# RWKV scan: products over four tiles of the array, copies for additions, and a first product in two parts

## The chip, the core and the metric

One core of a Trainium2 chip runs the whole program. The time is that of the device in microseconds, the median of three runs. The profile is one further execution of the same kernel, with a time of its own.

## What is computed

Two transformer blocks over 256 latent and 256 context tokens at width 1024, in fp32. The change lies in the second block's RWKV mixer: 8 heads of 64 channels, two directions, 512 tokens. Its recurrence, over tokens:

```python
def wkv7_scan(state0, r, w, k, v, a_vec, b_vec, reverse):
    xs = tuple(t.transpose(1, 0, 2, 3) for t in (r, w, k, v, a_vec, b_vec))

    def step(S, inp):
        r_t, w_t, k_t, v_t, a_t, b_t = inp
        sa = jnp.einsum('bhij,bhj->bhi', S, a_t)
        S = (S * w_t[:, :, None, :] + sa[..., None] * b_t[:, :, None, :]
             + v_t[..., None] * k_t[:, :, None, :])
        return S, jnp.einsum('bhij,bhj->bhi', S, r_t)

    s_fin, ys = lax.scan(step, state0, xs, reverse=reverse)
    return s_fin, ys.transpose(1, 0, 2, 3)
```

The kernel doesn't step through tokens. It takes 128 tokens at once: the matrix M of a chunk (how token s acts on token t, strictly triangular) enters as the inverse of (1 - M), and this inverse is built by halves: for blocks of width 1, 2, 4, ..., 64, with X the inverse so far, X becomes X + X (M masked to this level) X. There are seven levels.

## The kernel before

`Rwkv` (from L2434) has 32 units of work: 4 chunks of 128 tokens, times 4 pairs of heads, times 2 directions (`todo`). `run` (L2674) is called once for each engine and writes out that engine's queue by hand: a loop over rounds, where every fifth round (`APART`) starts a unit, and each running unit, oldest first, issues one round's share of its work. Four units run at a time (`NS`), each with a set of buffers. A unit of phase p stands in its round p. So queues are strictly in the order round, then age of the unit, and a wait at the head of a queue holds the other three units' work too.

A unit's rounds: ScalarE forms the decays EB and EI (phase 1); VectorE forms RA and KB (2); TensorE forms four matrices, KB against RA, 64x128 tiles of 256 columns, and transposes KB (3); VectorE masks the products into MM (`copy_predicated`, L173), ScalarE takes the diagonal blocks out as MC (3). Then the levels, i = 0 to 6: in phase 4 + 2i TensorE forms T = ML^T X0 (ML is MC masked by GpSimd), ScalarE copies T to T1, and in phase 5 + 2i TensorE forms T1^T X1 and X1^T T1 (the group called xx), which VectorE adds to XX, the pair of the inverse X0 and its transpose X1. The last level joins the two 64-token halves (XF). Then wu0 (16), wu1 (18), the state's update st and the output y (19). VectorE scales the state by the chunk's decay and writes y.

Two heads lie in the two halves of the partitions. Every 64x64 product of a level reads one half and writes the same half, so the groups use two of the array's four 64x64 tiles. PSUM's eight banks are given in turn (`Banks.take`, L251), and `free` makes TensorE wait until the bank's former content was read. `close_*` (L2698) end the readout of a pair of heads from round 146 on (`CLOSE`).

The level's products before:

```python
for hh in range(2):
    for b in both:
        ins = e.matmul(ps[b, hh * 64:(hh + 1) * 64], ML[b, hh, :], XX[b, 0, hh, :] if i else self.IC[b, :], True, True)
```

Of the kernel before, what the change touches and what calls it, by code (L numbers as in the profile page):

```python
# [240 lines left out]
class Banks:  # L241


    def __init__(self, tiles):
        self.tiles, self.n, self.bank, self.before, self.emptied = tiles, 0, {}, {}, {}
        self.inside = [None] * len(tiles)

    def again(self):
        self.n, self.inside = 0, [None] * len(self.tiles)

    def take(self, key):  # L251
        assert not Flag.counting[0] or key not in self.bank, key
        b = self.n % len(self.tiles)
        self.n += 1
        self.bank[key], self.before[key] = b, self.inside[b]
        self.inside[b] = key
        return self.tiles[b]

    def free(self, key):
        k = self.before[key]  # L260
        if k is None or Flag.counting[0]:
            return []
        return self.emptied[k]

    def of(self, key):
        return self.tiles[self.bank[key]]

# [73 lines left out]
class Kit:  # L341


    def __init__(self, nc, dram, outer):
# [5 lines left out]
        self.banks = Banks([outer.enter_context(nc.psum_tensor(f"ps{i}", [P, 512], F32)) for i in range(8)])  # L350
# [2083 lines left out]
class Rwkv:  # L2434
# [18 lines left out]
    def late(self, st):  # L2453
# [15 lines left out]
        size = dict(EB=[P, 129], RA=[P, 256], KBt=[P, 2, P], MM=[P, 2, 512], WU=[P, 2, P], XF=[P, 2, P], XX=[P, 2, 2, 64],  # L2469
                    T1=[P, 2, 64], sm=[P, 3])  # L2470
        self.sets, at = [{}], 0
        for k, s in size.items():
            n = int(np.prod(s[1:]))
            view = self.A[:, at:at + n]
            self.sets[0][k] = view if len(s) == 2 else view.rearrange("p (a n) -> p a n", a=2) if len(s) == 3 else \
                view.rearrange("p (a b n) -> p a b n", a=2, b=2)
            at += n
# [3 lines left out]
        for B in self.sets:  # L2481
            B["MC"], B["ML"] = (B["WU"][:, q, :].rearrange("p (h n) -> p h n", h=2) for q in range(2))
            B["EI"] = B["T1"].rearrange("p a n -> p (a n)")
            B["KB"] = B["XX"].rearrange("p q h n -> p q (h n)")
# [62 lines left out]
    def pe(self, e, beside, amid):  # L2547
# [29 lines left out]
        S.meet(e, p, "prep")  # L2577
        self.run(e, self.unit_pe, self.close_pe, amid)
        S.meet(e, p)
# [78 lines left out]
    def pool(self, e):  # L2658
# [3 lines left out]
        for b in (slice(0, 64), slice(64, 128)):  # L2662
# [5 lines left out]
            e.wait_ge(*o.now())  # L2668
        for B in self.sets:
            e.memset(B["XF"][:, :, :], 0.0).then_inc(*o.up("compact"))  # L2670
        self.run(e, self.unit_pool)
        S.meet(e, S.pool)

    def run(self, e, unit, close=None, beside=None):  # L2674


        running, closing = [], []
        for r in range(self.CLOSE[-1] + 4):
# [3 lines left out]
            for u in list(running):  # L2682
                if next(u, "over") == "over":
                    running.remove(u)
            assert len(running) <= self.NS
# [5 lines left out]
            if beside is not None:  # L2691
                beside(e, r)

# [87 lines left out]
    def unit_pe(self, e, n, step, d, j, B):  # L2781
# [6 lines left out]
        yield  # L2788
        yield
        yield  # L2790
        got = []
        for hh in range(2):
            got.append(g.banks.take(("mm", n, hh)))
            for tok in g.banks.free(("mm", n, hh)):
                e.wait_ge(*tok)
        e.wait_ge(*S.dve.at(("kb", n)))
        for q in range(2):
            for hh, b in enumerate(both):
                ins = e.matmul(got[hh][:, q * 256:(q + 1) * 256], KB[b, q, :], RA[b, :], True, True)
                if q:  # L2800
                    ins.then_inc(*p.up(("mm", n, hh)))
# [6 lines left out]
        yield  # L2808
        for i, li in self.levels():
            yield  # L2810
            key = ("lev", n, i)
            ps = g.banks.take(key)
            for tok in g.banks.free(key):
                e.wait_ge(*tok)
            if i:
                e.wait_ge(*S.dve.at(("x", n, i - 1)))
            if li:
                e.wait_ge(*S.pool.at(("ml", n, i)))
                e.wait_ge(*S.pool.at("compact"))
                for hh in range(2):  # L2820
                    for b in both:
                        ins = e.matmul(ps[b, hh * 64:(hh + 1) * 64], ML[b, hh, :], XX[b, 0, hh, :] if i else self.IC[b, :], True, True)
            else:
                for hh in range(2):
                    ins = e.matmul(ps[dst, hh * 64:(hh + 1) * 64], MM[src, hh, dst], XX[src, 0, hh, :], True, True)
            ins.then_inc(*p.up(("t", n, i)))
            if li == 0:
                self.wu0_pe(e, n, RA, MM, state, v)
            if i:
                yield  # L2830
                key = ("xx", n, i)
                ps = g.banks.take(key)
                for tok in g.banks.free(key):
                    e.wait_ge(*tok)
                e.wait_ge(*S.act.at(("t", n, i)))
                if li:
                    for hh in range(2):
                        for b in both:
                            e.matmul(ps[b, 128 + hh * 64:192 + hh * 64], T1[b, hh, :], XX[b, 1, hh, :], True, True)
                    for hh in range(2):  # L2840
                        for b in both:
                            ins = e.matmul(ps[b, hh * 64:(hh + 1) * 64], XX[b, 1, hh, :], T1[b, hh, :], True, True)
# [3 lines left out]
                ins.then_inc(*p.up(("x", n, i)))  # L2846
        yield
# [4 lines left out]
        e.wait_ge(*S.dve.at(("x", n, len(LEVELS) - 1)))  # L2852
# [3 lines left out]
        yield  # L2856
        u = WU[:, 1, :]
        e.wait_ge(*S.act.at(("wu1", n)))
        if step < 3:
            ps = g.banks.take(("st", n))  # L2860
            for tok in g.banks.free(("st", n)):
                e.wait_ge(*tok)
            e.wait_ge(*S.act.at(("kbt", n)))
            e.matmul(ps[:, 0:P], KBt[:, 0, :], u, True, False)
            e.matmul(ps[:, 0:P], KBt[:, 1, :], v, False, True).then_inc(*p.up(("st", n)))
        ps = g.banks.take(("y", n))
        for tok in g.banks.free(("y", n)):
            e.wait_ge(*tok)
        e.matmul(ps[:, 0:P], state, RA[:, P:2 * P], True, False)
        for hh, b in enumerate(both):  # L2870
            e.matmul(ps[b, 0:P], u[:, b], MM[:, hh, 128:256], False, False)
        for hh, b in enumerate(both):
            ins = e.matmul(ps[b, 0:P], v[:, b], MM[:, hh, 384:512], False, True)
        ins.then_inc(*p.up(("y", n)))

    def wu0_pe(self, e, n, RA, MM, state, v):
# [4 lines left out]
        e.wait_ge(*S.dve.at(("ts", n)))  # L2881
        e.matmul(ps[:, 0:P], RA[:, 0:P], state, True, False)
# [4 lines left out]
    def unit_act(self, e, n, step, d, j, B):  # L2887
# [4 lines left out]
        EB, EI, KBt, T1, WU, sm = (B[k] for k in ("EB", "EI", "KBt", "T1", "WU", "sm"))  # L2892
        src, dst = self.halves(d)
        two = lambda ap: ap.rearrange("p (h n) -> p h n", h=2)
        yield
        if n >= self.NS:
            e.wait_ge(*S.pe.at(("y", n - self.NS)))
            e.wait_ge(*S.dve.at(("end", n - self.NS)))
        e.activation(sm[:, 0:1], mc, ACT.Copy, scale=self.DECAY).then_inc(*a.up())
        e.activation(sm[:, 2:3], mc, ACT.Copy, scale=-self.DECAY).then_inc(*a.up())  # L2900
        e.wait_ge(*a.now())
        e.activation(EB[:, e0:e0 + P], cu, ACT.Exp, scale=-self.DECAY, bias=sm[:, 0:1]).then_inc(*a.up())
        e.activation(EI[:, :], cu, ACT.Exp, scale=self.DECAY, bias=sm[:, 2:3]).then_inc(*a.up())
        e.activation(sm[:, 1:2], mc, ACT.Exp, scale=-self.DECAY).then_inc(*a.up())
        x0 = 0 if d == 0 else 128
        e.activation(EB[:, x0:x0 + 1], mc, ACT.Exp, scale=self.DECAY).then_inc(*a.up(("eb", n)))
        yield
        yield
        e.wait_ge(*S.dve.at(("mk", n)))
        for b in (slice(0, 64), slice(64, 128)):  # L2910
            e.activation(B["MC"][b, :, :], B["MM"][b, :, b], ACT.Copy).then_inc(*a.up(("mc", n)))
# [3 lines left out]
        yield  # L2915
        for i, li in self.levels():
            yield
            if i:
                e.wait_ge(*S.pe.at(("t", n, i)))
                rows = slice(0, P) if li else dst  # L2920
                e.activation(T1[rows, :, :], two(g.banks.of(("lev", n, i))[rows, 0:128]), ACT.Copy).then_inc(*a.up(("t", n, i)))
                g.banks.done(("lev", n, i), a.now())
                if li == 0:
                    e.wait_ge(*S.pe.at(("wu0", n)))
                    e.activation(WU[:, 0, :], g.banks.of(("wu0", n))[:, 0:P], ACT.Copy).then_inc(*a.up(("wu0", n)))
                    g.banks.done(("wu0", n), a.now())
                yield
        yield
# [3 lines left out]
        yield  # L2932

    def unit_dve(self, e, n, step, d, j, B):
# [7 lines left out]
        yield  # L2942
        yield
# [5 lines left out]
        e.tensor_tensor(KB[:, 0, :], self.BB[d][:, j, cc], EI[:, :], MUL).then_inc(*v.up())  # L2949
        e.tensor_tensor(KB[:, 1, :], self.KD[d][:, j, cc], EI[:, :], MUL).then_inc(*v.up(("kb", n)))  # L2950
        e.wait_ge(*v.now())
        e.tensor_scalar(state, state, sm[:, 1:2], None, MUL).then_inc(*v.up(("ts", n)))
        yield
        mask = mid(g.C(f"tri{d}").bitcast(U32), 2, 256)
        for hh in range(2):
            e.wait_ge(*S.pe.at(("mm", n, hh)))
            e.wait_ge(*S.pool.at(("mz", n)))
            e.copy_predicated(two(MM[:, hh, :]), mask, two(g.banks.of(("mm", n, hh))[:, :])).then_inc(*v.up(("mk", n)))
            g.banks.done(("mm", n, hh), v.now())
        yield  # L2960
        for i, li in self.levels():
# [1307 lines left out]
```

## Time and profile before

| | us |
|---|---|
| median of three runs | 2538.28 (2536.87 to 2542.72) |
| the profiled execution | 2542.52, span 2540.7 |
| scan, from the first masks to the last product | about 1405 to 1757 of the span |
| busy over the span: TensorE, VectorE, ScalarE, GpSimd | 2341.8, 1744.4, 1051.7, 337.2 |

The span runs from the first to the last instruction. Each fp32 matmul stands in the trace as two records, and matmuls are pipelined, so start to start tells their cost and not their duration. Names are those of buffers: rwXX, rwMM, rwWU, rwT and so on are a unit's set; the first set lies in one tile, rwa, and a part of another in nv. rwWU holds MC and ML too, rwXX holds KB, rwT holds EI.

### The profile page before, as it was taken

To read this page: it belongs to the slowest core of one execution; us is meant where nothing else is said; L and a number is where in the kernel's file an instruction comes from. 1 tells how busy PE (TensorE), PEld (TensorE's weight loads), DVE (VectorE), ACT (ScalarE), POOL (GpSimd) and SP (SyncE) were. 2 spreads that over 40 slices of the span, in tenths; PEclk is the share of its full clock that TensorE was granted. 3 is DMA by queue.
4 is the path that set the end of the run, shared out by engine and by line. 5 is a ranking of instruction groups with operands and counts; after the bars stand their busy time and mean duration, and the time that the engine had idled before them with its cause. 6 is when DMAs were issued, how large, how long until landed. Compare 5 with 4: busy or idle time off the path is not lost.

```text
span 2540.7 us, 38727 instructions
## 1 busy us (share of the span) xinstructions
PE 2341.8 (92%) x15014; PEld 1751.2 (69%) x15014; DVE 1744.4 (69%) x3348; ACT 1051.7 (41%) x2068; POOL 337.2 (13%) x534
## 2 busy tenths in 40 slices
PE   7999999799989799989999899989999998998997
PEld 3788887465788799944454677775676775667775
DVE  4875687677756687834758666665678885748995
ACT  4222212224231434423134344442477773446884
POOL 0111110010001011000200233331011210001210
PEclk9999999899999899989998999999899999999998
DMA  8566654242226478711111000000389982126995
GB/s 307 190 204 199 216 197 161 94 141 91 101 74 206 142 265 269 254 43 66 39 43 35 18 3 3 2 3 26 109 286 341 324 314 108 59 70 216 338 339 188
DMA packets 114919, 386.47 MB, mean 152 GB/s; under 512 B 20144, under 2 KB 22320, under 8 KB 114480
## 3 DMA queue, kind: packets, MB, share of 16 engines
q1 hardware_dynamic: 76496, 275.81, 31.2%
q0 software_dynamic: 34848, 95.47, 11.3%
q10 hardware_dynamic: 3392, 12.72, 1.3%
q8 instruction: 119, 1.95, 0.3%
q14 instruction: 64, 0.52, 0.1%
HBM read 389.16 MB, written 26.21 MB: 163 GB/s over the span
## 4 chain that ended last, share of the span: by engine, by line
PE 37%; DVE 13%; DMA 8%; ACT 5%; issue 3%; POOL 0%; DVEq 0%; ACTq 0%; SPq 0%; POOLq 0%
PE ps L144 35%; DMA RG<-in_w 5%; DVE moe0wl L153 2%; PE ps L147 2%; DVE moe1wl L153 2%; DMA AR<-in_a 2%; DVE rwMM L173 1%; DVE f2wl L153 1%; DVE acc L161 1%; ACT moe0wh L150 1%; DVE H L161 1%; ACT moe1wh L150 1%; DVE rwXF L153 1%; ACT rwWU L150 1%; DVE rwXX L153 0%
## 5 line engine op out<-in xcount | busy, mean ns | idle before, releaser
L144 PE MATMUL ps<-H,RG 128*128 128x256 f32 (+2 forms) x1088 | 359.4, 491 | 14.0 <-ACT H L150 14.0
L161 DVE SCALAR_TENSOR_TENSOR acc<-AR,cs,acc 128x512 f32<-128x512 f32 x420 | 295.5, 746 | 48.9 <-DMA AR<-in_a 46.7
L144 PEld LDWEIGHTS ps<-H,RG 128*128 128x128 f32 (+1 forms) x1088 | 206.1, 194 | 149.8 <-issue 132.5
L153 DVE TENSOR_TENSOR moe0wl<-RG,moe0wh 128x1024 fp32r<-128x1024 f32 x144 | 173.6, 1219 | 42.8 <-ACT moe0wh L150 33.1
L150 ACT ACTIVATE moe0wh<-RG 128x1024 fp32r<-128x1024 f32 x144 | 150.8, 1061 | 73.9 <-DMA RG<-in_w 44.5
L200 POOL DMA_DIRECT2D AR<-in_a x152 | 82.1, 540 | 698.8 <-DVE acc L161 512.5
L150 ACT ACTIVATE f1wh<-RG 128x1024 fp32r<-128x1024 f32 x66 | 69.7, 1060 | 230.0 <-PE ps L144 229.9
L153 DVE TENSOR_TENSOR moe1wl<-RG,moe1wh 128x1024 fp32r<-128x1024 f32 x120 | 144.2, 1219 | 23.9 <-ACT moe1wh L150 19.8
L144 PE MATMUL ps<-f1hh,f1wh 128*128 128x512 f32 x352 | 142.5, 405 | 4.8 <-DVE f1hl L153 4.8
L150 ACT ACTIVATE moe1wh<-RG 128x1024 fp32r<-128x1024 f32 x120 | 125.9, 1060 | 46.8 <-DMA RG<-in_w 28.4
L144 PE MATMUL ps<-f1hl,f1wh 128*128 128x512 f32 x352 | 140.8, 400 | 0.0
L144 PE MATMUL ps<-f1hh,f1wl 128*128 128x512 f32 x352 | 140.7, 400 | 0.0
L153 DVE TENSOR_TENSOR f1wl<-RG,f1wh 128x1024 fp32r<-128x1024 f32 x66 | 80.4, 1221 | 54.8 <-ACT f1wh L150 53.1
L144 PE MATMUL ps<-f2hh,f2wh 128*128 128x256 f32 x352 | 103.2, 293 | 9.7 <-DVE f2hl L153 5.0
L144 PE MATMUL ps<-f2hh,f2wl 128*128 128x256 f32 x352 | 101.5, 288 | 0.0
L144 PE MATMUL ps<-f2hl,f2wh 128*128 128x256 f32 x352 | 101.4, 288 | 0.0
L150 ACT ACTIVATE f2wh<-RG 128x1024 fp32r<-128x1024 f32 x66 | 68.5, 1055 | 47.9 <-PE ps L144 47.9
L144 PE MATMUL ps<-moe0wh,moe0xh 128*128 128x512 f32 x184 | 78.6, 427 | 9.4 <-DVE moe0wl L153 9.3
L153 DVE TENSOR_TENSOR rwXX<-rwXX,ps 128x256 f32<-128x256 f32 (+1 forms) x120 | 47.1, 393 | 58.1 <-PE ps L144 57.5
L144 PE MATMUL ps<-rwa 64*64 64x64 f32 (+3 forms) x1228 | 74.5, 236 | 12.1 <-DVE rwa L153 5.6
L153 DVE TENSOR_TENSOR f2wl<-RG,f2wh 128x1024 fp32r<-128x1024 f32 x66 | 80.3, 1219 | 7.8 <-ACT f2wh L150 7.7
L144 PEld LDWEIGHTS ps<-f1hh,f1wh 128*128 128x128 f32 x352 | 68.6, 195 | 20.4 <-DVE f1hl L153 6.2
(633 smaller groups left out, 5742.3 us busy)
## 6 DMA issues: line engine op xcount, KB each, us to landing
RG<-in_w SPq DMA_DIRECT2D x524, 512.0 KB
AR<-in_a POOLq DMA_DIRECT2D x152, 512.0 KB, 3.9
moe0back<-moe_outs ACTq DMA_DIRECT2D x4, 1024.0 KB, 8.0
CT<-in_consts ACTq DMA_DIRECT2D x1, 2562.0 KB, 14.9
X<-in_x ACTq DMA_DIRECT2D x1, 2048.0 KB, 11.5
moe_rows<-moe0ht POOLq DMA_DIRECT2D x4, 512.0 KB, 5.4
moe1back<-moe_outs ACTq DMA_DIRECT2D x2, 1024.0 KB, 5.8
X<-in_ctx ACTq DMA_DIRECT2D x1, 1024.0 KB, 5.8
```

The source lines that it names most:

```text
L144: return Silent() if self.e is None else self.e.matmul(out, lhs, rhs, start=start, stop=stop, skip_group_check=True)
L147: return Silent() if self.e is None else self.e.transpose(out, x, ident)
L150: return Silent() if self.e is None else self.e.activation(out, x, f, **k)
L153: return Silent() if self.e is None else self.e.tensor_tensor(out, a, b, op)
L161: return Silent() if self.e is None else self.e.scalar_tensor_tensor(out=out, in0=a, scalar=s, in1=b, op0=op0, op1=op1)
L173: return Silent() if self.e is None else self.e.copy_predicated(out, mask, data)
L200: return Silent() if self.e is None else self.e.dma_start(out, src)
```

## The change

All of it is in the scan and in the allocation of PSUM banks.

- A round has four slots. Each engine's share of a unit is placed by (round, slot) in place of one share a round.
- T and X1^T T1 (level 0 to 5, and 1 to 5) are written so that the second head's product lands in the other half of the partitions: four products over the four tiles, into a pair of banks. XX is [P, 4, 64]: X0 of both heads, X1 of both.
- VectorE adds the identity to T while it copies it to T1, so xx gives the new X0 and X1 whole, and they are copied: one part by VectorE, three by ScalarE.
- The four matrices come in two parts, q = 0 in phase 2 and q = 1 in phase 3, with a mask after each. The transposes (kbt) move to phase 4.
- y and st share bank 7, kept for them, and half of their products are issued two rounds earlier (17); wu0 stands ahead of T6. The other products take seven banks in turn.
- At level 0 X0 is formed by a transposing product with the identity, X1 by GpSimd. GpSimd fills MM with identity and zeros. The last copies into XF are ScalarE's.
- The state's update comes in phase 20 and ahead of y's copy (21).

```diff
+    def take_pair(self, key):
+        self.n += self.n % self.turning == self.turning - 1
+        b = self.n % self.turning
+        self.n += 2
+        self.hold(key, [b, b + 1])
+        return self.tiles[b], self.tiles[b + 1]
...
+        g.banks.turning = 7
         self.run(e, self.unit_pe, self.close_pe, amid)
...
+    SLOTS = 4
...
+            for _ in range(self.SLOTS):
+                for u in list(running):
+                    if next(u, "over") == "over":
+                        running.remove(u)
...
     def unit_pe(self, e, n, step, d, j, B):
+        yield from to(2, 2)
+        self.mm_pe(e, n, 0, KB, RA)
+        yield from to(3, 2)
+        self.mm_pe(e, n, 1, KB, RA)
+        yield from to(4, 2)
         ps = g.banks.take(("kbt", n))
...
         for i, li in self.levels():
+            r = 4 + 2 * i if i else 5
+            if i == 6:
+                yield from to(r, 0)
+                self.wu0_pe(e, n, RA, MM, state, v)
+            yield from to(r, 1)
             key = ("lev", n, i)
+            ps = g.banks.take_pair(key) if li else g.banks.take(key)
...
+                for k, b in enumerate(both):
+                    for hh in range(2):
+                        ins = e.matmul(ps[hh][both[k ^ hh], 0:64], ML[b, hh, :], XX[b, 1 - hh, :], True, True)
...
+                yield from to(r + 1, 1)
                 key = ("xx", n, i)
+                ps = g.banks.take_pair(key) if li else g.banks.take(key)
...
+                        other, ps = g.banks.take(("xf", n)), ps[::-1]
...
+                    for k, b in enumerate(both):
+                        for hh in range(2):
+                            ins = e.matmul(ps[hh][both[k ^ hh], 0:64], XX[b, 2 + hh, :], T1[b, hh, :], True, True)
+                    ins.then_inc(*p.up(("x0", n, i)))
...
+        yield from to(17, 3)
+        out = g.banks.take(("y", n), 7)
...
+        yield from to(18, 0)
         ps = g.banks.take(("wu1", n))
...
+        yield from to(19, 3)
...
     def unit_dve(self, e, n, step, d, j, B):
+        yield from to(2, 1)
...
+        e.tensor_tensor(KB[:, 0, :], self.BB[d][:, j, cc], EI[:, :], MUL).then_inc(*v.up(("kb", n, 0)))
+        yield from to(3, 0)
+        e.tensor_tensor(KB[:, 1, :], self.KD[d][:, j, cc], EI[:, :], MUL).then_inc(*v.up(("kb", n, 1)))
+        masks(0)
+        yield from to(3, 2)
         e.tensor_scalar(state, state, sm[:, 1:2], None, MUL).then_inc(*v.up(("ts", n)))
+        yield from to(4, 2)
+        masks(1)
...
+                yield from to(4 + 2 * i, 1)
+                e.wait_ge(*S.pe.at(("t", n, i)))
+                e.tensor_tensor(T1[:, :, :], g.banks.pair(("lev", n, i))[:, :, 0:64], one, ADD).then_inc(*v.up(("t", n, i)))
...
+                yield from to(5 + 2 * i, 1)
...
+                    e.tensor_copy(XX[:, 0, :], new[:, 1, 0:64]).then_inc(*v.up(("x0", n, i)))
```

## Rows read from the trace of the kernel before

**Rows 1.** The page: the span, and busy time of each engine.
```profile
span 2540.7 us, 38727 instructions
...
PE 2341.8 (92%) x15014; PEld 1751.2 (69%) x15014; DVE 1744.4 (69%) x3348; ACT 1051.7 (41%) x2068; POOL 337.2 (13%) x534
```
**Rows 2.** Table by stage, steady scan: busy us (records) PE PEld DVE ACT POOL, clock, DMA.
```profile
1504.05:1605.20 101.15, 93.03 (x1701) 78.41 (x1701) 65.65 (x211) 41.63 (x171) 34.91 (x71) 1.00 0.01 2
```
**Rows 3.** The chain of waits over the scan: start, us, what.
```profile
1443.34 3.51 PE ps L144 x60
...
1564.74 3.51 PE ps L144 x60
1568.25 1.34 DVE rwa L173 x2
...
1686.10 3.51 PE ps L144 x60
```
**Rows 4.** Order of time, TensorE, one period: start us, us, line, out<-in, tile, moving.
```profile
1564.74 0.45 PE L144 MATMUL ps<-rwXX,rwWU 64*64 64x64 f32 x8 [0.24 <-DVE rwXX L153]
1565.02 0.40 PE L144 MATMUL ps<-rwXX,nv 64*64 64x64 f32 x8
1565.26 0.40 PE L144 MATMUL ps<-nv,rwXX 64*64 64x64 f32 x8
...
1567.06 1.13 PE L144 MATMUL ps<-rwa 64*128 64x256 f32 x8
1568.13 0.44 PE L147 MATMUL ps<-CT,rwa 128*128 128x128 f32 x2
1568.40 0.39 PE L144 MATMUL ps<-rwWU,rwKBt 128*128 128x128 f32 x2
...
1569.17 0.44 PE L144 MATMUL ps<-rwMM,rwWU 128*64 128x128 f32 x4
...
1569.75 0.45 PE L144 MATMUL ps<-rwXX,rwWU 64*64 64x64 f32 x8
...
1572.46 0.44 PE L144 MATMUL ps<-rwXX,rwMM 64*64 64x64 f32 x4 [0.37 <-DVE rwXF L153]
1572.84 0.49 PE L144 MATMUL ps<-rwst,rwRA 128*128 128x128 f32 x2
...
1573.65 0.45 PE L144 MATMUL ps<-rwXX,nv 64*64 64x64 f32 x8
```
**Rows 5.** The same, TensorE, where two units' groups meet.
```profile
1574.28 0.22 PE L144 MATMUL ps<-rwXF,rwT 64*64 64x64 f32 x1
1574.29 0.27 PE L144 MATMUL ps<-rwa 64*64 64x64 f32 x2
1574.34 0.22 PE L144 MATMUL ps<-rwXF,rwT 64*64 64x64 f32 x1
1574.35 0.22 PE L144 MATMUL ps<-rwa 64*64 64x64 f32 x1
```
**Rows 6.** The same, VectorE, one period.
```profile
1565.70 0.42 DVE L153 TENSOR_TENSOR rwXX<-rwXX,ps 128x256 f32<-128x256 f32 x1 [0.69 <-PE ps L144]
1566.04 0.29 DVE L161 SCALAR_TENSOR_TENSOR rwa<-rwkk,rwa 128x128 f32<-128x128 f32 x1
1566.25 0.29 DVE L153 TENSOR_TENSOR rwa<-abr,rwa 128x128 f32<-128x128 f32 x1
...
1570.08 0.46 DVE L153 TENSOR_TENSOR rwst<-rwst,ps 64x64 f32<-64x64 f32 x2
1570.57 0.29 DVE L158 TENSOR_SCALAR rwst<-rwst,rwEB 128x128 f32<-128x128 f32 x1
```
**Rows 7.** The same, ScalarE, one period.
```profile
1569.61 0.65 ACT L150 ACTIVATE rwa<-rwa 64x128 f32<-64x128 f32 x2 [2.15 <-DVE rwa L173]
1570.28 0.39 ACT L150 ACTIVATE rwa<-ps 128x256 f32<-128x256 f32 x1
1570.56 0.27 ACT L150 ACTIVATE rwT<-ps 128x128 f32<-128x128 f32 x1
```

More of the change, by code:

```diff
@@ L241, with __init__, hold, take @@
 class Banks:
-    def __init__(self, tiles):
-        self.tiles, self.n, self.bank, self.before, self.emptied = tiles, 0, {}, {}, {}
-        self.inside = [None] * len(tiles)
+    def __init__(self, whole):
+        self.whole, self.tiles = whole, [whole[:, i, :] for i in range(8)]
+        self.bank, self.before, self.emptied = {}, {}, {}
+        self.again()
     def again(self):
-        self.n, self.inside = 0, [None] * len(self.tiles)
-    def take(self, key):
+        self.n, self.inside, self.turning = 0, [None] * len(self.tiles), len(self.tiles)
+    def hold(self, key, banks):
         assert not Flag.counting[0] or key not in self.bank, key
[L253 to L256, printed above, removed]
-        return self.tiles[b]
+        self.bank[key], self.before[key] = banks[0], [self.inside[b] for b in banks]
+        for b in banks:
+            self.inside[b] = key
+    def take(self, key, kept=None):
+        b = self.n % self.turning if kept is None else kept
+        self.n += kept is None
+        self.hold(key, [b])
+        return self.tiles[b]
+    def take_pair(self, key):
[4 more added lines that the diff above has]
+        return self.tiles[b], self.tiles[b + 1]
     def free(self, key):
-        k = self.before[key]
-        if k is None or Flag.counting[0]:
+        if Flag.counting[0]:
             return []
-        return self.emptied[k]
+        return [tok for k in self.before[key] if k is not None for tok in self.emptied[k]]
     def of(self, key):
         return self.tiles[self.bank[key]]
+    def pair(self, key):
+        return self.whole[:, self.bank[key]:self.bank[key] + 2, :]
     def done(self, key, *toks):
@@ L349, in __init__ @@
         self.CL, self.VL, self.ncst = CL, VL, ncst
-        self.banks = Banks([outer.enter_context(nc.psum_tensor(f"ps{i}", [P, 512], F32)) for i in range(8)])
+        self.banks = Banks(outer.enter_context(nc.psum_tensor("ps", [P, 8, 512], F32)))
         sb = self.sb
@@ L2668, in pool @@
             e.wait_ge(*o.now())
+        for d in range(2):
+            e.tensor_tensor(self.LC[d][:, 5, :], self.LC[d][:, 5, :], self.IC[:, :], ADD).then_inc(*o.up())
+            e.wait_ge(*o.now())
         for B in self.sets:
@@ L2692, in run, with clock, to @@
                 beside(e, r)
+    def clock(self):
+        at = [0]
+        def to(r, slot):
+            for _ in range(r * self.SLOTS + slot - at[0]):
+                at[0] += 1
+                yield
+        return to
     def last(self, j):
@@ L2787, in unit_pe @@
         src, dst = self.halves(d)
[L2788 to L2801, printed above, removed]
+        to = self.clock()
+        yield from to(2, 2)
[3 more added lines that the diff above has]
+        yield from to(4, 2)
         ps = g.banks.take(("kbt", n))
@@ L2836, in unit_pe @@
                 if li:
+                    other = ps[0]
+                    if li == 1:
+                        other, ps = g.banks.take(("xf", n)), ps[::-1]
+                        for tok in g.banks.free(("xf", n)):
+                            e.wait_ge(*tok)
+                    for k, b in enumerate(both):
+                        for hh in range(2):
+                            ins = e.matmul(ps[hh][both[k ^ hh], 0:64], XX[b, 2 + hh, :], T1[b, hh, :], True, True)
+                    ins.then_inc(*p.up(("x0", n, i)))
@@ L2837, in unit_pe @@
                     for hh in range(2):
                         for b in both:
[L2839 to L2842, printed above, removed]
+                            ins = e.matmul(other[b, 64 + 64 * hh:128 + 64 * hh], T1[b, hh, :], XX[b, 2 + hh, :], True, True)
@@ L2845, in unit_pe @@
                         ins = e.matmul(ps[src, hh * 64:(hh + 1) * 64], T1[dst, hh, :], XF[dst, hh, dst], True, True)
-                ins.then_inc(*p.up(("x", n, i)))
-        yield
+                ins.then_inc(*p.up(("x1", n, i)))
+        yield from to(17, 3)
+        out = g.banks.take(("y", n), 7)
+        for tok in g.banks.free(("y", n)):
+            e.wait_ge(*tok)
+        e.wait_ge(*S.dve.at(("ts", n)))
+        e.matmul(out[:, 0:P], state, RA[:, P:2 * P], True, False)
+        if step < 3:
+            e.wait_ge(*S.act.at(("kbt", n)))
+            e.matmul(out[:, P:2 * P], KBt[:, 1, :], v, False, False)
+        yield from to(18, 0)
         ps = g.banks.take(("wu1", n))
@@ L2851, in unit_pe @@
         e.wait_ge(*S.act.at(("wu0", n)))
[L2852 removed]
+        e.wait_ge(*S.dve.at(("xf", n)))
         for hh in range(2):
@@ L2859, in unit_pe, with mm_pe @@
         if step < 3:
[L2860 to L2867, printed above, removed]
-            e.wait_ge(*tok)
[L2869 to L2874, printed above, removed]
+            e.matmul(out[:, P:2 * P], KBt[:, 0, :], u, False, True).then_inc(*p.up(("st", n)))
+        for hh, b in enumerate(both):
+            e.matmul(out[b, 0:P], u[:, b], MM[:, hh, 128:256], False, False)
+        for hh, b in enumerate(both):
+            ins = e.matmul(out[b, 0:P], v[:, b], MM[:, hh, 384:512], False, True)
+        ins.then_inc(*p.up(("y", n)))
+    def mm_pe(self, e, n, q, KB, RA):
+        g, p, S = self.g, self.S.pe, self.S
+        got = g.banks.take_pair(("mm", n, q))
+        for tok in g.banks.free(("mm", n, q)):
+            e.wait_ge(*tok)
+        e.wait_ge(*S.dve.at(("kb", n, q)))
+        for hh, b in enumerate((slice(0, 64), slice(64, 128))):
+            ins = e.matmul(got[hh][:, 0:256], KB[b, q, :], RA[b, :], True, True)
+        ins.then_inc(*p.up(("mm", n, q)))
     def wu0_pe(self, e, n, RA, MM, state, v):
@@ L2941, in unit_dve, with masks @@
         two = lambda ap: ap.rearrange("p (h n) -> p h n", h=2)
-        yield
-        yield
+        mask, T1 = mid(g.C(f"tri{d}").bitcast(U32), 2, 256), B["T1"]
+        to = self.clock()
+        def masks(q):
+            e.wait_ge(*S.pe.at(("mm", n, q)))
+            e.wait_ge(*S.pool.at(("mz", n)))
+            e.copy_predicated(MM[:, :, q * 256:(q + 1) * 256], mask, g.banks.pair(("mm", n, q))[:, :, 0:256]).then_inc(*v.up(("mk", n, q)))
+            g.banks.done(("mm", n, q), v.now())
+        yield from to(2, 1)
         if n >= self.NS:
@@ new lines, in unit_dve @@
+        yield from to(20, 0)
+        if step < 3:
+            last = e0 + (P - 1 if d == 0 else 0)
+            e.wait_ge(*S.pe.at(("st", n)))
+            e.wait_ge(*S.pe.at(("y", n)))
+            e.wait_ge(*v.at(("ts", n)))
+            for lo in (0, 64):
+                q = slice(lo, lo + 64)
+                e.tensor_tensor(state[q, q], state[q, q], g.banks.of(("y", n))[q, P + lo:P + lo + 64], ADD).then_inc(*v.up())
+            e.wait_ge(*v.now())
+            e.tensor_scalar(state, state, EB[:, last:last + 1], None, MUL).then_inc(*v.up())
+            v.note(("end", n))
+            yield from to(21, 0)
@@ L2997, in unit_dve @@
         g.banks.done(("y", n), v.now())
[L2998 to L3008 removed]
+        if step == 3:
+            v.note(("end", n))
     def unit_pool(self, e, n, step, d, j, B):
```

202 lines of the change are left out of this document (89 added, 113 removed).

## The prediction, made before the changed kernel ran

> **What bounds the kernel now.** I read the page first: TensorE is busy 92% of the span, so no other engine is the bound over the whole [rows 1]. The change touches only the RWKV scan, so I cut the scan's steady stretch out with the table by stage: in 101.15 us TensorE shows 93 us of busy time, VectorE 66, ScalarE 42 and GpSimd 35, at a granted clock of 1.00 of full speed and with no DMA to speak of [rows 2]. The chain of waits then shows the rhythm: the same piece of 60 matmul records comes back every (1686.10 - 1443.34) / 24 = 10.115 us [rows 3]. That is one unit, since the round loop starts a unit every five rounds and there are 32. One period's chain has 3.51 us of TensorE in one run and then 1.34 us of masks on VectorE [rows 3]; copies on ScalarE and two more pieces of TensorE with their handoffs make the rest. So TensorE's in-order queue sets the end, but it isn't full: it stands still for VectorE's XF before the row of 1572.46 [rows 4], and at three more such places of the period, some 1.4 us together as I add them up from start to start. What decides is the order of the queues, not busy time.
>
> **Products over four tiles.** A level product is four 64x64 products, eight records (two for each fp32 product). On two tiles eight records take 0.24 us from start to start (1565.02 to 1565.26), which is 0.058 us for each step of two; the first step after a stop takes 0.05 more (1564.74 to 1565.02 is 0.28) [rows 4]. Do four tiles go at once? Before has no such group, but one nearest case: a product in a third tile (rwXF) starts inside a group on the two others: records of both start at 1574.28, 1574.29, 1574.34 and 1574.35, so three tiles keep the 0.058 step [rows 5]. I take two steps, 0.12 us, for a product over four; the bounds are 0.12 and the 0.24 of now. This holds for T at levels 0 to 5 and the first half of xx at 1 to 5: 11 groups a unit, 11 x 0.12 = 1.3 us less TensorE work a period.
>
> The Trainium skill (TensorE: Matmul & The Clock Gate, "Wait — 56ns, not 53.3ns?") says that matmuls never start closer than about 25 ns. By that, eight records take 0.20 us and not 0.12, and the change saves a third of this. Rows 5 speak against it.
>
> **Copies in place of additions.** VectorE's addition over 256 columns (0.42) [rows 6] becomes an addition of 128 columns into T1 (0.29, taken as the scaling of 1570.57) and a copy of 64 columns (0.22, half of the 0.46 of two 64x64 ones) [rows 6]. ScalarE's T1 copy (0.27) [rows 7] becomes a copy of 192 columns, which I put at 0.33, between the 0.27 of 128 and the 0.39 of 256 [rows 7]. ScalarE also gets the four quarters of XF (4 x 0.245, from the same rows) and four MC copies in place of two, 1.2 us for 0.65 [rows 7]; its work grows from 4.2 to about 6.4 us a period, still under 10. GpSimd loses a quarter of the memset and gets a copy and two half products: under 5 us, and nobody waits for it in what follows.
>
> **Where it is put.** Four slots a round reorder the queues, and here I have to walk one period. t = 0 is the first record of x5 (xx of level 5) of the oldest unit; T and x carry the level number. Units of phases 15, 10 and 5 meet in this round, 16, 11, 6 in the next, and so on. A result is read 0.26 after the start of its last 64-column record (0.22 and 0.04), 0.32 after one of 128; back to TensorE costs 0.05. Ready VectorE operations follow each other at 0.20 for 128 columns (1566.04 to 1566.25) [rows 6]. A change of the tile's shape costs 0.09 ahead and 0.05 on the first record, an estimate from 1569.17 to 1569.75, 0.58 for eight records that make four steps of 0.11 [rows 4].
>
> Banks come first. The change takes them in turn from 7, in pairs for products over four tiles. In the order of TensorE's queue a period takes x5 2, xf 1, T3 2, T0 2, wu0 1, T6 1, x3 2, T1 2, x6 1, T4 2, x1 2, mm0 2, wu1 1, x4 2, T2 2, mm1 2, T5 2, x2 2, kbt 1. Counted out (a pair skips bank 6), every starting bank leads to a period that starts at bank 3 and stays there. Then T0 gets a bank of x5, which was taken one group before, and kbt gets the first bank of mm1, free only after mask 1. Both are waits at the head of TensorE's queue, with everything of the other units behind them.
>
> - 0 to 1.27: x5 and T3 are issued by 0.51. T0 waits for the bank of x5. VectorE's queue has the state first: it starts at 0.12, when y is there, and takes two additions and a scaling, 0.79 (1570.08 to 1570.57, plus 0.29) [rows 6], then x5's copy, 0.3: T0 at 1.27.
> - 1.27 to 2.83: T0 0.17 with its stop, wu0 0.81 (1572.84 to 1573.65) [rows 4] and 0.09 for the change of shape, T6's four records in one tile (0.22 to the last start), and 0.26 to its reader.
> - 2.83 to 3.55: ScalarE copies T6, wu0 and x3 in this order, 0.19 apart and 0.33 for the last. x6 waits for the second (its bank), T4 for the third.
> - 3.55 to 3.82: T4, then the first half of x1.
> - 3.82 to 5.15: x1 is read after 0.26; VectorE copies it and only then forms RA (two) and KB0, 0.2 apart and 0.29 for the last, for these stand last in the same slot. mm0 waits for KB0: TensorE idle 1.04.
> - 5.15 to 8.28: TensorE in one run: mm0 0.62 (half of the 1.07 of 1567.06 to 1568.13, and a change), the early half of y and st 0.50 and wu1 0.44 (records of 0.11) [rows 4], x4 0.60 with its change, T2 0.12, mm1 0.62, T5 0.17, the first half of x2. VectorE's mask 0 (0.7) is hidden by x4 and T2; MC and its copies, which are on today's chain, are hidden by T5 to y.
> - 8.28 to 9.54: x2 is read after 0.26, VectorE copies it (0.23), then mask 1 (0.72, half of the 1.34 pair with its tail) [rows 3]; only then does kbt get its bank. TensorE idle 0.97.
> - 9.54 to 10.70: kbt 0.27 (1568.13 to 1568.40), the late half of st 0.23, and y with two changes of shape 0.66 (1569.17 to 1569.75 and 0.09) [rows 4].
>
> The period is 10.70 against 10.12 us: TensorE has 1.3 us less of level products (0.3 comes back as two more changes of shape), but stands still for about 3.2 us where now it is about 1.4. The gain is real and is spent at mm0, T0 and kbt. What is late next if T0's wait goes is T6's copy, behind EB on ScalarE.
>
> **The sum.** Of the 31 intervals between units 24 are steady and 4 at the start nearly so; the last three hold the closing of the readout and I leave them alone. 28 x 0.58 = +16 us. In the drain, where one or two units are left, a level costs 0.12 less for T and about 0.2 less for xx (two steps and 0.09 of the copy): 6 x 0.3, -2 us. Together +14. The profiled execution took 2542.5 us (span 2540.7), 4.2 over the median of the three timed runs; on it the sum is 2556.5, on the median 2552.5, and the latter is my forecast.
>
> **Bounds.** If VectorE's operations don't overlap where I let them (0.3 instead of 0.2, some five places on the walk) the period is 11.2, +28; if the changes of shape are hidden behind the stops and handoffs cost 0.02 (as mask to copy in rows 3 and 7, 1569.59 to 1569.61), 10.3, +3. This case alone: 2541 to 2566. Measuring can tell about 0.2% (5 us) from no change.
>
> **The rivals.**
> 1. Faster: the walk is wrong about one of the two long waits, at mm0 (1.04) or at kbt (0.97). Then the period is 9.7, 28 x -0.42 - 2 = -14: 2524. It decides as soon as a period falls under 10.0, and so needs 0.7 us of my 10.7 to be cover. For it: today's chain carries 1.34 of masks and the ScalarE copies behind them, which do leave it. Against it: both waits follow from the order of the diff alone. Chance 0.17.
> 2. Much faster: both waits are hidden, period 8.7, -42: 2496. Chance 0.10.
> 3. No change: the walk is 0.3 to 0.7 too long in many small places: 2533 to 2543. Chance 0.13.
> 4. The change doesn't do what it says: four tiles go no faster than two. Seven such groups lie on the walk's path, 7 x 0.12 = 0.8, period 11.5, +37: 2575. Against it rows 5. Chance 0.08. (The 25 ns of the Trainium skill's page named above would put it at 0.08 a group, +30.)
>
> **How the numbers follow.** My forecast has 0.52: 2552.5. The range reaches from half-way between rivals 1 and 2 to the end of rival 4: 2510 to 2574, which leaves out most of rival 2 and the upper half of rival 4. Faster is rivals 1 and 2, 0.27; same is rival 3, 0.13; slower 0.60. The clock is no case of its own: TensorE loses 1.0 us of work in 10 and the shorter stops are spread over the period, and it stood at 1.00 here [rows 2].
>
> **What would show it.** The masks of following units should stand 10.7 us apart, in halves. The 64x256 products should have about 1 us of TensorE idle time before half of them, ended by VectorE's KB (rwXX); the transposes (L147) about 1 us, ended by the mask; T0 0.7, ended by a copy of VectorE. The eight records of a level product should take 0.12 us and 0.05 after a stop. It would be wrong if mask 1 ends before x2 is issued, if the transposes follow x2 without a gap, or if the period is under 10 with all of these stops in place, which would mean that my TensorE pieces are too long.

## The result, and the profile after

The changed kernel takes 2587.12 us (median of four runs, 2575.0 to 2603.28) against 2540.5 for the kernel before on the same chip: 1.019 times as long, 95% interval 1.013 to 1.025. The profiled execution is the second slowest of the four, 2593.69 us. My 2552.5 had the right sign, but the time lies outside my range, which ended at 2574.

The page of after: the span, the busy time of each engine, and TensorE and its granted clock in 40 slices of 65 us.

```profile
span 2591.9 us, 38979 instructions
...
PE 2341.6 (90%) x15014; PEld 1732.5 (67%) x15014; DVE 1727.4 (67%) x3380; ACT 1101.3 (42%) x2260; POOL 350.0 (14%) x600
...
PE   7999999799989799899998877778899998998996
...
PEclk9999999899999899999998699997999999998998
```

TensorE's busy time is what it was (2341.8, [rows 1]), although 11 groups a unit should cost half. The slices 22, 23 and 28 show why this proves nothing: there the clock has an 8, a 6 and a 7, and records are longer. The table by stage separates the two. Columns: stretch, busy us (records) of PE, PEld, DVE, ACT and POOL, granted clock, DMA share and GB/s.

```profile
1440.00:1455.00 15.00, 13.40 (x168) 10.36 (x168) 5.56 (x22) 5.63 (x23) 3.88 (x9) 0.50 0.00 1
1455.00:1470.00 15.00, 13.54 (x170) 10.90 (x169) 5.77 (x22) 5.78 (x23) 3.87 (x9) 0.50 0.00 1
...
1500.00:1583.00 83.00, 62.70 (x1296) 49.54 (x1292) 45.02 (x165) 43.34 (x178) 29.62 (x69) 1.00 0.01 2
...
1662.00:1678.00 16.00, 13.26 (x198) 10.28 (x198) 6.90 (x28) 6.12 (x25) 4.55 (x11) 0.68 0.01 3
```

At full clock TensorE is busy for 62.70 of 83 us, 76%, where it was 92% [rows 2]: its work did shrink. But there are stretches at 0.50, the lower of the clock's two levels (1.2 GHz), with 11 records per us in place of 16. The chain of waits shows a unit's piece of TensorE coming back (start, us, what).

```profile
1453.49 5.79 PE ps L144 x47
...
1469.22 5.80 PE ps L144 x47
...
1519.33 3.31 PE ps L144 x46
...
1530.29 3.31 PE ps L144 x46
...
1541.28 3.31 PE ps L144 x46
...
1815.31 35.03 PE ps L144 x81
```

A period is (1541.28 - 1519.33) / 2 = 10.98 us at full clock, against 10.12 [rows 3], and 1469.22 - 1453.49 = 15.73 at 0.50. The low clock time of a stretch is 2 x (1 - clock) x length. Added up over the scan in stages such as those above it is 112.6 us for after and 6.8 for before. The distance from the first unit's mask to the last one's is 378.2 us, 31 x 10.98 = 340.4 and 37.8 more; before it is 318.7, 31 x 10.12 = 313.7 and 5.0 more. Call what goes beyond 31 periods the surplus. Before's 5.0 are not the clock: its low clock lies behind the last unit's mask, and the 5.0 come from the first and last three distances, which are 10.2 to 12.2 us long. After has 101 of its 112.6 us between the two masks. In the period, a us of the low level costs 1 - 10.98 / 15.73 = 0.30 us, so 101 x 0.30 = 30 of the 33 us by which the surplus grew.

So of the 51 us between the two spans, 27 are the longer period (31 x 0.86), 33 the larger surplus, 30 of them by the low clock. The masks begin 6 earlier, and the rest nearly cancels: +5 from the last mask to the long block of 1815.31, TensorE's work that follows the last unit, and -7 behind it. The four timed runs agree in kind: their granted clocks over the whole span, 0.959, 0.958, 0.949 and 0.943, go with 2575.0, 2580.56, 2593.69 and 2603.28 us.

One period of after, TensorE in order of time (start, us, line, out<-in, tile, moving, idle before):

```profile
1519.33 0.70 PE L144 MATMUL ps<-rwRA,rwXX 64*128 64x256 f32 x4 [0.82 <-DVE rwXX L153]
...
1523.77 0.44 PE L147 MATMUL ps<-CT,rwXX 128*128 128x128 f32 x2 [0.83 <-DVE rwMM L173]
...
1524.95 0.34 PE L144 MATMUL ps<-nv,rwXX 64*64 64x64 f32 x8
1525.12 0.33 PE L144 MATMUL ps<-rwXX,nv 64*64 64x64 f32 x5
...
1526.36 0.34 PE L144 MATMUL ps<-rwa,rwXX 64*64 64x64 f32 x8 [0.72 <-ACT rwXF L150]
...
1528.40 0.44 PE L144 MATMUL ps<-rwXF,nv 64*64 64x64 f32 x4 [0.23 <-ACT rwWU L150]
1528.67 0.34 PE L144 MATMUL ps<-rwa 64*64 64x64 f32 x8
...
1530.29 0.49 PE L144 MATMUL ps<-rwRA,rwXX 64*128 64x256 f32 x2 [0.93 <-DVE rwXX L153]
```

The three long stops are there: mm0 (0.93) for VectorE's KB, the transposes (0.83) for the mask, T0 (0.72). T0's releaser is given as ScalarE's rwXF. VectorE's rows of the same moment name another:

```profile
1525.14 0.47 DVE L153 TENSOR_TENSOR rwst<-rwst,ps 64x64 f32<-64x64 f32 x2 [1.42 <-PE ps L144]
1525.64 0.29 DVE L158 TENSOR_SCALAR rwst<-rwst,rwEB 128x128 f32<-128x128 f32 x1
1525.96 0.29 DVE L164 COPY rwXX<-ps 128x128 f32<-128x128 f32 x1
```

The state goes first, x5's copy ends at 1525.96 + 0.29 = 1526.25, and T0 starts 0.11 later. ScalarE is still copying XF then (0.94 us from 1525.56, until 1526.50). Four tiles are fast: from x5's first record to the next group 0.17 us.

### The profile page after: what moved, and what is told of

It is laid out like the page before. It is cut to its first block, busy times and chain, and to the rows that moved or that the text cites. A ratio compares the mean times of both kernels' runs of the same rounds, so it can differ in the third digit from the quotient of the medians.

```text
span 2591.9 us, 38979 instructions
## 1 busy us (share of the span) xinstructions
PE 2341.6 (90%) x15014; PEld 1732.5 (67%) x15014; DVE 1727.4 (67%) x3380; ACT 1101.3 (42%) x2260; POOL 350.0 (14%) x600
## 4 chain that ended last, share of the span: by engine, by line
PE 37%; DVE 13%; DMA 8%; ACT 5%; issue 3%; POOL 0%; DVEq 0%; ACTq 0%; SPq 0%; POOLq 0%
PE ps L144 35%; DMA RG<-in_w 6%; DVE moe0wl L153 2%; PE ps L147 2%; DVE moe1wl L153 2%; DMA AR<-in_a 1%; DVE f2wl L153 1%; DVE acc L161 1%; ACT moe0wh L150 1%; ACT moe1wh L150 1%; DVE rwMM L173 1%; DVE H L161 1%; DMA moe0back<-moe_outs 0%; ACT rwXF L150 0%; ACT rwa L150 0%
## 5 line engine op out<-in xcount | busy, mean ns | idle before, releaser
L150 ACT ACTIVATE rwa<-ps 128x192 f32<-128x192 f32 (+5 forms) x119 | 38.5, 324 | 110.8 <-PE ps L144 90.5
```

The source lines that it names most:

```text
L150: return Silent() if self.e is None else self.e.activation(out, x, f, **k)
```

## Experiments

Each is the kernel of the change with one edit, unless it says otherwise. "Period" is the distance between masks of following units at full clock; "low clock" is the time at 0.50 in the scan of the profiled execution, added up as above, in us.

| run | median, us | against before on its chip | period | low clock |
|---|---|---|---|---|
| after_again | 2576.53 | 1.018 (1.016 to 1.020) | 10.99 | 48 |
| double | 2597.37 | 1.026 (1.024 to 1.028) | 11.55 | 14 |
| fill | 2578.21 | 1.016 (1.014 to 1.018) | 10.99 | 55 |
| early_both | 2527.01 | 0.997 (0.996 to 0.999) | 9.47 | 41 |
| early_kb | 2562.95, one run | | 10.07 | 68 |
| early_mask | 2560.34, one run | | 10.35 | 55 |
| late_state | 2573.58, one run | | 10.37 | 82 |
| early_state | 2510.65 | 0.990 (0.989 to 0.992) | 8.86 | 27 |
| before_stop | 2649.11 | 1.045 (1.043 to 1.047) | 11.65 | 167 |
| stop_filled | 2594.81 | 1.023 (1.020 to 1.026) | 11.65 | 10 |
| drain_fill | 2507.4 | 0.989 (0.986 to 0.992) | 8.86 | 10 |

**after_again**, the changed kernel once more, beside the three that follow.

> The changed kernel once more, beside the others on one chip. Theory A (stops, then clock): between units 10.98 us wherever the granted clock is 1.00, as in the first profile, 15 to 16 us where it is 0.50; the time moves with the share of low clock, 2570 to 2605. Theory B (the low clock of the first profile was a chance of that execution): no stretch of 0.50 longer than 10 us in the scan, and 2560 to 2570.

Measured: 1.018 (1.016 to 1.020), period 10.99, but 48 us at low clock instead of 113. The scan's masks span 356.0 us, 31 x 10.98 and a surplus of 15.6. Of the low clock 31 us lie between them, and 31 x 0.30 = 9 of the 11 us over before's surplus. The period belongs to the program. How much of the scan runs at the low level differs between runs of the same program, and the price of 0.30 a us accounts for most of both surpluses.

**double**: is the product over four tiles as cheap as I took it?

```diff
-                for k, b in enumerate(both):
-                    for hh in range(2):
-                        ins = e.matmul(ps[hh][both[k ^ hh], 0:64], XX[b, 2 + hh, :], T1[b, hh, :], True, True)
+                for _ in range(2):
+                    for k, b in enumerate(both):
+                        for hh in range(2):
+                            ins = e.matmul(ps[hh][both[k ^ hh], 0:64], XX[b, 2 + hh, :], T1[b, hh, :], True, True)
```

(and the same for T). 

> Every product over four tiles (T at levels 0 to 5, first half of xx at 1 to 5) is issued twice, with the same result: 11 x 0.12 = 1.3 us more TensorE work a unit. Theory A: at full clock the period grows by the seven groups on the path, 0.8 us, to 11.8; TensorE is busier, so there is less low clock, and the two nearly cancel: 2575 to 2600. Theory B (the clock has nothing to do with the work done): 28 x 0.8 = 23 us over the changed kernel, about 2610. If four tiles went no faster than two, the period would grow by 1.6.

TensorE and two masks of double:

```profile
1510.16 0.46 PE L144 MATMUL ps<-nv,rwXX 64*64 64x64 f32 x16
1510.44 0.33 PE L144 MATMUL ps<-rwXX,nv 64*64 64x64 f32 x5
```

```profile
1509.24 0.74 DVE L173 COPY_PREDICATED rwMM<-CT,ps 128x512 f32<-128x512 uint32 x1 [0.60 <-PE ps L144]
...
1520.73 0.73 DVE L173 COPY_PREDICATED rwMM<-CT,ps 128x512 f32<-128x512 uint32 x1 [0.60 <-PE ps L144]
```

Eight more records of x5 cost 0.28 - 0.17 = 0.11 us, the two steps of 0.058 of my sum, 14 ns a record. The masks stand 11.48 and 11.62 us apart in turn, so all 11 groups doubled add 11.55 - 10.98 = 0.57 to the period. Seven on my path would be 0.8; part of them lies under the waits, which are shorter here (T0's 0.48 for 0.72, mm0's 0.71 for 0.82 and 0.93). Rival 4 falls. The run also has less low clock, 14 us, with more work in each period. It is slower all the same.

**fill**: keep TensorE busy in one of the three stops, ahead of mm0, with constants into the banks that mm0 then overwrites.

```diff
+        if q == 0:
+            for cols in (256, 128):
+                for hh, b in enumerate((slice(0, 64), slice(64, 128))):
+                    e.matmul(got[hh][:, 0:cols], g.C("ones")[b, :], g.C("lev0")[b, 0:cols], True, True)
```

> Four matrices' first part: while TensorE stands still for KB0, it forms products of constants into the two banks that the real product overwrites (0.65 us of a stop of about 0.95). No other work moves. Theory A: the period at full clock stays at 11.0 (at most 11.15), and the stretches of clock 0.50 in the scan shrink: 15 to 35 us under the changed kernel. Theory B: the same or slower by up to 5 us.

TensorE of fill, where mm0's stop was:

```profile
1534.69 0.93 PE L144 MATMUL ps<-CT 64*128 64x256 f32 x8
1535.58 0.70 PE L144 MATMUL ps<-rwRA,rwXX 64*128 64x256 f32 x4
```

The stop is filled and the period unchanged, but the low clock isn't less (55 us) and the time is that of after_again. My expectation failed. The stops of 0.83 and 0.72 remained. Most of the 55 us lie at the scan's start and end: between 1500 and 1725 fill has 3.4 us at the low level, after 17 and after_again 10, and the four falls of these two in that stretch begin 0.1 to 0.3 us behind mm0's stop, the one that fill closes. That points to the stop, but late_state below keeps it and has no low clock there at all, so one profile of each settles nothing. before_stop and stop_filled put the question more plainly.

**early_both, early_kb, early_mask**: RA and KB0 are formed two slots earlier, ahead of x1's copy instead of behind it; mask 1 goes two slots earlier too, ahead of x2's copy. Each edit also alone.

```diff
-        yield from to(2, 1)
+        yield from to(1, 3)
...
-        yield from to(4, 2)
+        yield from to(4, 0)
         masks(1)
```

> Two placements undone: VectorE forms RA and KB0 in slot (1, 3), ahead of the next round's copies, and takes mask 1 in slot (4, 0), ahead of T5 and x2. Theory A: the stops at the first four-matrix product (0.95) and at the transposes (0.97, of which 0.5 is left to the mask itself) shrink, the period at full clock is 9.4 to 9.7, under the 10.12 of before, and the clock falls less: 2505 to 2535. Theory B: the same period, but the clock's loss stays: 2540 to 2555. If the stops were cover for other waits, the period stays above 10.5.

> Of the two placements of early_both only the first: RA and KB0 in slot (1, 3). From the walk: the stop before the first four-matrix product goes, 0.95 us, and nothing else takes its place: 10.0 a period at full clock. If the two stops cover each other, 10.5 or more.

> Only the second: mask 1 in slot (4, 0). The transposes still wait for the mask itself (0.72 after the product), so about 0.55 of the 0.97 goes: 10.4 a period at full clock. If the bank weren't what they wait for, 10.98 as in the changed kernel.

TensorE's stops of over 0.2 us in one period of early_both, and two masks:

```profile
1519.88 0.44 PE L144 MATMUL ps<-rwXF,rwT 64*64 64x64 f32 x4 [0.26 <-ACT rwWU L150]
1524.60 0.44 PE L147 MATMUL ps<-CT,rwXX 128*128 128x128 f32 x2 [0.22 <-DVE rwMM L173]
1527.18 0.34 PE L144 MATMUL ps<-rwa,rwXX 64*64 64x64 f32 x8 [0.72 <-ACT rwXF L150]
```

```profile
1521.52 0.74 DVE L173 COPY_PREDICATED rwMM<-CT,ps 128x512 f32<-128x512 uint32 x1
...
1531.03 0.72 DVE L173 COPY_PREDICATED rwMM<-CT,ps 128x512 f32<-128x512 uint32 x1
```

The stop at mm0 is gone, that at the transposes is 0.22, and T0's is untouched. (One period has 9.51 us, the next 9.41, mean over the steady part 9.47.) The stop at mm0 is worth 10.98 - 10.07 = 0.91 a period, that behind mask 1 10.98 - 10.35 = 0.63, and both 1.51. Two lines of order carry the kernel from 1.8% slower to 0.3% faster, at the same products and copies. The two single runs are slower than their periods alone would make them (2563 at 10.07); both have over 50 us at low clock, and with one run each their times aren't weighed further.

**late_state, early_state**: the third stop. The state's update moves behind x5's copy, in the changed kernel alone and on top of early_both.

```diff
-        yield from to(20, 0)
+        yield from to(20, 2 if step < 3 else 0)
```

> The changed kernel with only the state's update moved, to slot (20, 2). T0 and what follows come 0.5 to 0.6 earlier: 10.4 to 10.5 a period at full clock, as early_state against early_both (9.47 to 8.86). If the other two stops take the gain up, 10.9 or more.

> early_both, and the state's update in slot (20, 2), behind x5's copy and T3's addition. The stop before T0 (0.8 to 0.9) shrinks by 0.5: 8.9 to 9.1 a period at full clock against 9.47. The share of TensorE's work rises, so if the clock follows the work, there is no more low clock than in early_both, and 2508 to 2520. If T0 waits for ScalarE's XF copies and not for VectorE, the period stays at 9.4 to 9.5 and the time at 2527.

Three masks of the same half in early_state:

```profile
1519.36 0.74 DVE L173 COPY_PREDICATED rwMM<-CT,ps 128x512 f32<-128x512 uint32 x1
...
1528.19 0.73 DVE L173 COPY_PREDICATED rwMM<-CT,ps 128x512 f32<-128x512 uint32 x1
...
1537.09 0.73 DVE L173 COPY_PREDICATED rwMM<-CT,ps 128x512 f32<-128x512 uint32 x1
```

Both times the period falls by 0.61 (10.98 to 10.37, 9.47 to 8.86). VectorE and ScalarE of late_state at T0, which starts there at 1526.14 with no stop over 0.2:

```profile
1525.75 0.29 DVE L164 COPY rwa<-ps 128x128 f32<-128x128 f32 x1 [1.65 <-PE ps L144]
```

```profile
1525.95 0.95 ACT L150 ACTIVATE rwa<-ps 64x64 f32<-64x64 f32 x4
```

T0 starts 0.10 after VectorE's copy of x5 and 0.76 before ScalarE's XF is done. So the stop was x5's bank behind the state on VectorE, as the walk had it, and not rwXF. early_state is 1.0% faster than before. Its low clock lies in the scan's end, where its periods are no longer steady.

**before_stop, stop_filled**: does the clock fall because TensorE stands still, or because of something in the change (four tiles, more ScalarE)? This is the kernel BEFORE, with each mask done twice over the same data; TensorE's work and every order stay as they were, and it stands still for longer. stop_filled then adds six rounds of constant 64x64 products before the wait of xx at level 5, overwritten by what follows.

```diff
+            e.copy_predicated(two(MM[:, hh, :]), mask, two(g.banks.of(("mm", n, hh))[:, :])).then_inc(*v.up())
+            e.wait_ge(*v.now())
             e.copy_predicated(two(MM[:, hh, :]), mask, two(g.banks.of(("mm", n, hh))[:, :])).then_inc(*v.up(("mk", n)))
```

```diff
+                if i == 5:
+                    for _ in range(6):
+                        for hh in range(2):
+                            for b in both:
+                                e.matmul(ps[b, hh * 64:(hh + 1) * 64], g.C("ones")[b, 0:64], g.C("lev0")[b, 0:64], True, True)
                 e.wait_ge(*S.act.at(("t", n, i)))
```

> The kernel before, with each of the two masks done twice in a row, so TensorE stands still 1.5 us longer in each period and its work is unchanged: 11.5 to 11.7 a period, about as long as the changed kernel's with 1.0 us more of TensorE work. Theory A in its stricter form (the clock falls because there is less work in the time, the four tiles' saving included): the clock stays at 1.00 but for under 15 us in the scan, 2575 to 2585. Theory C (stops alone bring it down, whatever the work): 40 us and more of 0.50 in the scan, 2590 to 2605.

> The kernel before_stop, and in its longest TensorE stop (1.8 us ahead of xx of level 5, until ScalarE's T1) six rounds of four products of constants (1.4 us) into the bank that the real products overwrite. The chain isn't touched. If the clock falls because TensorE does nothing for that long, it stays at 1.00: every period 11.6, and the time falls from 2649 to 2580 to 2595. If the clock follows anything else (VectorE's masks, the length of the period), periods still go between 11.6 and 15.6, and 2640 to 2655.

before_stop: two stages, TensorE's long stops, and the masks (x4, since each is done twice):

```profile
1440.00:1500.00 60.00, 49.58 (x769) 41.91 (x771) 34.96 (x103) 19.21 (x79) 17.14 (x35) 0.83 0.01 2
1500.00:1560.00 60.00, 51.44 (x729) 43.38 (x726) 34.31 (x100) 18.07 (x75) 14.51 (x29) 0.77 0.01 2
```

```profile
1507.09 0.45 PE L144 MATMUL ps<-rwXX,rwT 64*64 64x64 f32 x8 [1.74 <-ACT rwT L150]
...
1522.53 0.45 PE L144 MATMUL ps<-rwXX,nv 64*64 64x64 f32 x8 [1.34 <-ACT nv L150]
```

```profile
1502.91 2.87 DVE L173 COPY_PREDICATED rwa<-CT,ps 128x512 f32<-128x512 uint32 x4 [0.64 <-PE ps L144]
...
1518.33 2.90 DVE L173 COPY_PREDICATED rwMM<-CT,ps 128x512 f32<-128x512 uint32 x4 [2.00 <-PE ps L144]
...
1529.99 2.86 DVE L173 COPY_PREDICATED rwMM<-CT,ps 128x512 f32<-128x512 uint32 x4 [0.64 <-PE ps L144]
...
1544.29 2.88 DVE L173 COPY_PREDICATED rwMM<-CT,ps 128x512 f32<-128x512 uint32 x4 [1.02 <-PE ps L144]
```

stop_filled: the same stages and masks.

```profile
1440.00:1500.00 60.00, 54.63 (x1121) 47.16 (x1119) 40.48 (x119) 21.13 (x86) 17.48 (x35) 0.99 0.01 3
1500.00:1560.00 60.00, 55.04 (x1128) 47.59 (x1126) 40.59 (x118) 21.39 (x87) 18.70 (x38) 1.00 0.01 3
```

```profile
1505.67 2.88 DVE L173 COPY_PREDICATED rwa<-CT,ps 128x512 f32<-128x512 uint32 x4 [0.65 <-PE ps L144]
...
1517.33 2.90 DVE L173 COPY_PREDICATED rwMM<-CT,ps 128x512 f32<-128x512 uint32 x4 [0.65 <-PE ps L144]
...
1528.99 2.87 DVE L173 COPY_PREDICATED rwMM<-CT,ps 128x512 f32<-128x512 uint32 x4 [0.64 <-PE ps L144]
```

With such a stop in each period (about 1.74 us, or 1.34 to 1.67 in most periods that follow a stretch at low clock), and without anything of the change, the clock is at 0.83 and 0.77, the periods are 15.4, 11.7 and 14.3 us, and the kernel is 4.5% slower. Its 2649 us lie 44 above the top of what I had expected under the theory that came true, since I had not priced so much low clock. With the same stop filled (0.36 us of it are left) the periods shown are 11.66 and the clock is 1.00: TensorE does more work and the kernel is 54 us faster than before_stop; the two ran on different chips, where they took 1.045 (before_stop) and 1.023 times as long as before. So in this kernel it is TensorE standing still that brings the clock down, and useless products in the stop keep it up.

**drain_fill**: early_state with such constants ahead of the waits of the last three units, where its low clock lies.

```diff
+            if n >= 29 and i and li:
+                self.idle_pe(e, g, ps, both)
...
+    def idle_pe(self, e, g, ps, both):
+        for _ in range(3):
+            for k, b in enumerate(both):
+                for hh in range(2):
+                    e.matmul(ps[hh][both[k ^ hh], 0:64], g.C("ones")[b, 0:64], g.C("lev0")[b, 0:64], True, True)
```

> early_state, and for the last three units products of constants (0.35 us) ahead of the data wait of T (levels 1 to 5) and xx (1 to 4), in tiles and banks of their own. What low clock early_state has in the scan lies in the drain, 27 us. If idle TensorE is the cause there too: the last three periods (10.3, 12.4, 15.4) shorten to 9.5 to 12, and 2500 to 2508. If the products lie on the path of units that wait for results, they cost up to 10 x 0.35 = 3.5 us and the clock stays: 2511 to 2515.

The low clock falls from 27 to 10 us, but the last three periods, which I had wanted to shorten, are 10.3, 13.1 and 14.4 us for 10.3, 12.4 and 15.4. And 0.989 (0.986 to 0.992) can't be told from early_state's 0.990 (0.989 to 0.992). From the first mask to the long block behind the last unit it is 327.3 us for 326.2. So 17 us less of low clock gained nothing there in one profile each; whether the constants took the gain back isn't shown.

## Why the prediction was wrong

**The walk through the period held.** The pieces, from the rows of after against mine: x5 to T0 1.41 for 1.27; T0 to T4 2.31 for 2.28; T4 to mm0 1.62 for 1.60; mm0 to the transposes 4.44 for 4.39; from there to x5 1.18 for 1.16. The stops are at T0, mm0 and kbt for the reasons given, and taking them away one by one is worth 0.61, 0.91 and 0.63 (I had 0.76, 1.04 and 0.97). The period is 10.98 for 10.70, inside my 10.3 to 11.2. Half of the difference is T0's stop. On 28 periods that makes +24 us for my +16, and this alone would have left the time inside my range.

**Four tiles** cost 0.11 to 0.12 us, as taken from [rows 5]. The Trainium skill (TensorE: Matmul & The Clock Gate, "Wait — 56ns, not 53.3ns?") has about 25 ns as the least distance between matmuls. The 0.11 us for eight records in double, 14 ns each, show that this figure doesn't hold for products that go to different tiles.

**The rivals.** 1 and 2 needed one or both waits to be cover; early_kb and early_mask show that neither is. 4 falls with double. 3 needed a period near 10.1.

**The failed step** is the sentence "The clock is no case of its own". I argued that the loss of 1.0 us of work in 10 was small, that the stops were spread over the period, and that the clock stood at 1.00 in the kernel before [rows 2]. But that row shows a TensorE at 92%, and I had just worked out one that stands still for 3.2 of 10.7 us. A row of a fuller engine says nothing of the clock of an emptier one. This step was worth about 30 us in the profiled execution of after (101 us of low clock between the masks, in a surplus of 37.8 against 5.0) and 9 in after_again (31 us, 15.6 against 5.0): with it, and with the period, my sum would have been 2552.5 + 8 + (9 to 30) = 2570 to 2591. Two of the four runs lie in it (2575.0, 2580.56), the two with the lower granted clocks above it. The Trainium skill (the same page, "A second HAM failure mode: psum-queue depth-cycling") tells of a kernel whose TensorE idles shortly between groups as PSUM banks go round, and whose clock swings between its two levels. That is what after shows, 0.50 over 1440 to 1470 and 1.00 over 1500 to 1583, and I hadn't weighed it. I should have given the low clock a rival of its own.

**Also mis-sized**: the drain, the end of the scan in which units run out. I gave it -2 us. From the last unit's mask to the long block of 1815.31 the scan takes 37.2 us, against 32.6 before, and even early_state, whose steady part ran at full clock, has its 27 us of low clock there.

**What stays open**: what set of stops brings the clock down, and when. The same program had 113 and 48 us at the low level; double, with more work in the period, 14; fill, with one of three stops closed, 55; early_both, whose longest stop is T0's 0.72, still 41. So neither the number of long stops nor the work settles it here. That standing still is the cause is shown only for the longer stop of before_stop; that the falls in after have the same cause is the reading of the rows, and early_state, whose steady part has neither these stops nor a low clock, agrees in one profile. Since early_state keeps every product over four tiles and ScalarE's added copies, these alone don't bring the clock down in its steady part.

## What to carry to other kernels

Fewer products on a busy in-order engine are worth nothing until the queues behind them are reordered: walk one steady period, name each wait at the head of the engine's queue, and ask which operation of VectorE stands before the one waited for. Here three moves by two slots each turned 1.8% slower into 1.0% faster. And when a change leaves TensorE waiting for some us in ten, price the period at the lower clock as well; do not take the clock from the trace of the fuller kernel.

## What the hardware showed unexpectedly

With one stop of about 1.74 us in each period of 11.65, the granted clock went from 1.00 to 0.50 again and again (167 us of low clock in before_stop's scan). Between 1450 and 1780 each of its 13 falls began 1.3 to 2.1 us behind a stop of 1.72 to 1.76 us. Constant products put into that stop, of which 0.36 us were left, kept the clock at 1.00. A us at the low level cost the steady scan 0.30 us (period 10.98 at full clock, 15.73 at half), since part of the period is other engines' work. And the records of 64x64 products that rotate over four tiles start 14 ns apart on average (0.11 us for eight in double).
